# Three latent projections on the raw activations, and a wait moved at a second entry

## The reference, cut to what matters

```
h   = rms_norm(x, mix_norm_g)                       # x: 512 x 1024
cq, ckv, kr, dq, dk, dv, nq, nkv, ng = split(h @ w_in)
qm  = rms_norm(cq,  mla_q_norm_g)  @ mla_w_uq       # cq: 256 columns
kvm = rms_norm(ckv, mla_kv_norm_g) @ mla_w_ukv      # ckv: 128 columns
rms_norm(x, g) = x * rsqrt(mean(x * x) + 1e-6) * g
```

## Time and profile before

| | |
|---|---|
| time, median of three runs | 3802.02 us |
| the profiled execution, its own time | 3804.82 us |
| its span, first to last instruction | 3803.0 us |
| mean granted clock of TensorE | 0.968 |
| PE busy | 3590.6 us (94%) |
| DVE, ACT, POOL busy | 1340.9, 1271.8, 1412.2 us |

### The profile page before, as it was taken

One profiled execution on the slowest core, in us unless ns is written; L12 is line 12 of the kernel. 1 busy time (PEld: TensorE's weight loads), 2 busy tenths in 40 slices (PEclk: granted clock), 3 DMA queues, 4 the chain that ended last, 5 costly groups with the idle time before them and its releaser, 6 DMA issues. The chain is left out here.

```text
span 3803.0 us, 50606 instructions
## 1 busy us (share of the span) xinstructions
PE 3590.6 (94%) x18340; PEld 2846.2 (75%) x18340; DVE 1340.9 (35%) x1910; ACT 1271.8 (33%) x1998; POOL 1412.2 (37%) x756
## 2 busy tenths in 40 slices
PE   7999899999999999899999996999998997879998
PEld 6888675688887888666688885888886874648886
DVE  4233545552325223545542335111115204561112
ACT  4222434542224222334542233312123234234222
POOL 4444333344444444333344442322232440024443
PEclk9999999999999999999999998999998998889999
DMA  4333343233323333333233332222212321013331
GB/s 132 100 94 88 91 120 112 84 89 97 97 85 104 94 99 89 97 111 104 84 94 100 94 100 56 61 67 61 65 51 61 86 75 61 1 44 89 99 94 61
DMA packets 569026, 322.34 MB, mean 85 GB/s; under 512 B 30266, under 2 KB 563360, under 8 KB 568480
## 3 DMA queue, kind: packets, MB, share of 16 engines
q1 hardware_dynamic: 568864, 320.22, 28.9%
HBM read 318.08 MB, written 2.10 MB: 84 GB/s over the span
## 5 line engine op out<-in xcount | busy, mean ns | idle before, releaser
L866 POOL TENSOR_TENSOR w_lo<-w_raw,w_hi 128x1024 fp32r<-128x1024 f32 x516 | 1270.0, 2462 | 2135.1 <-ACT w_hi L911 2135.0
L911 ACT ACTIVATE w_hi<-w_raw 128x1024 fp32r<-128x1024 f32 x516 | 547.0, 1061 | 1847.7 <-PE psum L2143 1733.5
L2143 PE MATMUL psum<-h_hi,w_hi 128*128 128x512 f32 x1296 | 525.9, 406 | 59.5 <-DVE x_lat L1920 27.3
L2143 PE MATMUL psum<-xg_hi,w_hi 128*128 128x512 f32 x1408 | 551.7, 392 | 12.5 <-DVE xg_lo L1470 10.6
L2143 PE MATMUL psum<-xg_lo,w_hi 128*128 128x512 f32 x1408 | 549.0, 390 | 0.0
L2143 PE MATMUL psum<-xg_hi,w_lo 128*128 128x512 f32 x1408 | 548.8, 390 | 0.0
L2143 PE MATMUL psum<-h_lo,w_hi 128*128 128x512 f32 x1296 | 511.2, 394 | 0.0
L2143 PE MATMUL psum<-h_hi,w_lo 128*128 128x512 f32 x1296 | 511.1, 394 | 0.0
L2143 PE MATMUL psum<-a_hi,w_hi 128*128 128x512 f32 x1232 | 433.0, 375 | 4.9 <-DVE a_lo L1587 4.2
L2143 PE MATMUL psum<-a_hi,w_lo 128*128 128x512 f32 x1232 | 432.8, 374 | 0.0
L2143 PE MATMUL psum<-a_lo,w_hi 128*128 128x512 f32 x1232 | 432.3, 374 | 0.0
(11 more groups left out here) (448 smaller groups left out, 4329.7 us busy)
## 6 DMA issues: line engine op xcount, KB each, us to landing
w_raw<-ffn_w SPq DMA_DIRECT2D x120, 512.0 KB, 3.8
w_raw<-ffn_w_gate SPq DMA_DIRECT2D x88, 512.0 KB, 3.8
w_raw<-ffn_w_up SPq DMA_DIRECT2D x88, 512.0 KB, 3.8
ada_raw<-ada_w SPq DMA_DIRECT2D x72, 512.0 KB, 4.6
w_raw<-ffn_w_down SPq DMA_DIRECT2D x64, 512.0 KB, 4.1
w_raw<-w_in SPq DMA_DIRECT2D x60, 512.0 KB, 3.8
w_raw<-ffn_w_down SPq DMA_DIRECT2D x32, 384.0 KB, 3.4
w_raw<-w_out SPq DMA_DIRECT2D x24, 512.0 KB, 4.0
```

The costliest lines, as they stand in the source:

```text
L866: nc.gpsimd.tensor_tensor(w_lo[:, i, :], w_raw[:, i, :], w_hi[:, i, :].bitcast(F32), ALU.subtract).then_inc(lo_ready, 1)
L911: nc.scalar.activation(w_hi[:, pos, :], w_raw[:, pos, :], ACT.Copy).then_inc(hi_ready, 1)
L2143: last = nc.tensor.matmul(dst, w[:, pos, k * P:(k + 1) * P], rhs[g][r](k0 + k), start=k == 0 and m == 0, stop=k == nk - 1 and m == 2)
```

## The change

The mixer's norm gets the arrangement of the FFN: xg_high and xg_low (into a new buffer, mix_lo, that lies over parts of the FFN's buffers which are free by then) run beside the last down tiles. Tiles 0 to 2 (`RAW = 3`) are multiplied from xg. Tiles from the fourth (s = 3) read the normed h_hi and h_lo as before; ACT makes h_hi of chunks 0 to 3 behind tile 0 and of chunks 4 to 7 behind tile 1. The latents are then not normed, so epsilon in their own norms has to be multiplied by mean(x*x) + epsilon: PE adds that to banks 2 and 3 with latent_least times rstd (two matmuls and one) ahead of chunk 7 of tile 0, and the bias becomes epsilon squared. The wait for the parameter loads and for the sum of squares, and the norm's own sum, move to the same place. The clearing of taps moves, since its place now holds xg. In `ffn`, the wait for x_updated is left out in part 0. The rest is renumbering of semaphores.

```diff
 # buffers
+        mix_lo = (over("mix_lo_0", [P, 2, T], zone + 4 * (PARTS[-1][1] * T), F32R), over("mix_lo_1", [P, 6, T], zone + 4 * ((PARTS[0][1] + PARTS[-1][1]) * T), F32R))
+        latent_least = over("latent_least", [P, P], latents_at + 4 * 8 * T)
+        RAW = 3
...
 # ScalarE
-                    nc.scalar.activation(root, sums, ACT.Abs_reciprocal_sqrt, bias=eps[:, 0:1], scale=1.0 / width).then_inc(latent_std.sem, 1)
+                    nc.scalar.activation(root, sums, ACT.Abs_reciprocal_sqrt, bias=eps_square[:, 0:1], scale=1.0 / width).then_inc(latent_std.sem, 1)
...
+                    if s == 0:
+                        norm_high(layer, 1, [(h_hi, 0, T)], cs=range(KD // 2))
                     if s == 1:
...

+                        norm_high(layer, 1, [(h_hi, 0, T)], cs=range(KD // 2, KD))
...
-                late_ffn(layer, FFN_S0[0], FFN_N0[0], lambda c: square(layer, 1, MIX_Y0, c, rows))
-                norm_statistics(layer, 1, MIX_Y0, rows, KD - 1)
-                norm_high(layer, 1, [(h_hi, 0, T)])
+                def mixer_norm(c):
+                    xg_high(layer, 1, MIX_Y0, c, lambda c: layer_gains[:, GAIN_MIX + c:GAIN_MIX + c + 1])
+                    square(layer, 1, MIX_Y0, c, rows)
+
+                late_ffn(layer, FFN_S0[0], FFN_N0[0], mixer_norm)
+                xg_high(layer, 1, MIX_Y0, KD - 1, lambda c: layer_gains[:, GAIN_MIX + c:GAIN_MIX + c + 1])
+                norm_statistics(layer, 1, MIX_Y0, rows, KD - 1, 5)
...
 # VectorE
+                    if v == 0:
+                        nc.vector.memset(taps[:, :, :, NC:CMP_BLOCK], 0.0)
                     place(0, 1, psum[:, 2 + events % 2, :])
...
-                nc.vector.memset(taps[:, :, :, NC:CMP_BLOCK], 0.0)
...
-                    nc.vector.scalar_tensor_tensor(half_square, psum[:, 2 + n, :], width * EPS, half_square, ALU.add, ALU.mult).then_inc(turn_read.sem, 1)
+                    nc.vector.scalar_tensor_tensor(half_square, psum[:, 2 + n, :], width * EPS * EPS, half_square, ALU.add, ALU.mult).then_inc(turn_read.sem, 1)
...
                 def mixer_norm(c):
+                    if c == 0:
+                        nc.vector.memset(latent_least[:], -P * EPS / D)
+                    xg_low(layer, 1, c, lambda c: layer_gains[:, GAIN_MIX + c:GAIN_MIX + c + 1], mix_low(c))
                     if c:
                         norm_add(layer, 1, c, T)
 
                 late_ffn(layer, 0, FFN_S0[0], FFN_N0[0], FFN_Y0[0], mixer_norm)
-                norm_apply(layer, 1, lambda c, g: layer_gains[:, GAIN_MIX + c:GAIN_MIX + c + 1], lats)
+                xg_low(layer, 1, KD - 1, lambda c: layer_gains[:, GAIN_MIX + c:GAIN_MIX + c + 1], mix_low(KD - 1))
+                norm_apply(layer, 1, lambda c, g: layer_gains[:, GAIN_MIX + c:GAIN_MIX + c + 1], lats, 2, bank=5)
...
 # TensorE
-                            if len(groups) > 1:
+                            if len(groups) > 1 and part:
...
-                        last = nc.tensor.matmul(psum[:, b, :], ones[:], flat[:, c * T:(c + 1) * T], start=c == chunks[0], stop=c == chunks[-1])
+                        last = nc.tensor.matmul(psum[:, b, :], ones[:], flat[:, c * T:(c + 1) * T], start=False, stop=c == chunks[-1])
...
-                pe.wait_ge(*params_loaded(layer, PARAMS * 16))
-
-                pe.wait_ge(*x_updated(layer, MIX_Y0))
+                mix = (lambda k: xg_hi[:, k, :]), mix_low
+                mix_ready, normed_rows_ready = rows_ready(layer, 1), rows_ready(layer, 2)
+
+                def first_chunk(k):
+                    if k == KD - 1:
+                        pe.wait_ge(*params_loaded(layer, PARAMS * 16))
+                        pe.wait_ge(*sq_used(layer, 2 * (KD - 1)))
+                        for b, times in ((2, MLA_QR // P), (3, MLA_KVR // P)):
+                            for n in range(times):
+                                nc.tensor.matmul(psum[:, b, :], latent_least[:], rstd[:, 0:T], start=n == 0, stop=False)
+                        norm_sums(layer, 1, [(0, T)], 5)
+                    mix_ready(k)
+
                 for s in range(N_T):
...
-                    dense(s % SLOTS, 0, KD, [lat], [bank_of(s)], rows_ready(layer, 1) if s == 0 else None).then_inc(slot_used, 1)
+                    dense(s % SLOTS, 0, KD, [mix if s < RAW else lat], [bank_of(s)],
+                          first_chunk if s == 0 else normed_rows_ready if s == RAW else None).then_inc(slot_used, 1)
...
-                norm_sums(layer, 1, [(0, T)])
```

More of the change, by code:

```diff
@@ L417, in build @@
         normed_ready = signal("normed_ready", KD)
-        h_hi_ready = signal("h_hi_ready", NORMS * KD)
-        h_lo_ready = signal("h_lo_ready", NORMS * KD, 2)
+        h_hi_ready = signal("h_hi_ready", (NORMS + 1) * KD)
+        h_lo_ready = signal("h_lo_ready", (NORMS + 1) * KD, 2)
         scaled = signal("scaled", 4 * NF)
@@ L562, in slot_of, with mix_low @@
             return layer * (LAYER_SLOTS // SLOTS) + s // SLOTS, s % SLOTS
+        RAW = 3
+        def mix_low(c):
+            return mix_lo[0][:, c, :] if c < 2 else mix_lo[1][:, c - 2, :]
         LAT = [(0, 0, T)]
@@ L939, in norm_statistics, with norm_high @@
                                      scale=(0.5 / D) ** 0.5).then_inc(std_ready.sem, 1)
-            def norm_high(layer, v, groups, shift=None):
-                for c in range(KD):
+            def norm_high(layer, v, groups, shift=None, cs=range(KD)):
+                for c in cs:
                     act.wait_ge(*normed_ready(layer, (v * KD if shift else 0) + c + 1))
@@ L1465, in norm_add, with xg_low @@
                 last.then_inc(sq_used.sem, 1)
-            def xg_low(layer, v, c, gain):
+            def xg_low(layer, v, c, gain, low=None):
                 dve.wait_ge(*h_hi_ready(layer, v * KD + c + 1))
-                nc.vector.scalar_tensor_tensor(xg_lo[:, c, :], x_lat[:, c, :], gain(c), xg_hi[:, c, :].bitcast(F32),
+                nc.vector.scalar_tensor_tensor(xg_lo[:, c, :] if low is None else low, x_lat[:, c, :], gain(c), xg_hi[:, c, :].bitcast(F32),
                                                ALU.mult, ALU.subtract).then_inc(h_lo_ready.sem, 1)
@@ L1502, in _, with norm_apply @@
             nc.vector.tensor_reduce(cond_sum[:], ident[:].rearrange("p (k m) -> p m k", m=COND_M)[:, 0:2, :], AX_X, ALU.add).then_inc(cond_ready, 1)
-            def norm_apply(layer, v, gain, xs, u=None, shift=None, rooted=False):
+            def norm_apply(layer, v, gain, xs, u=None, shift=None, rooted=False, bank=0):
                 u = v if u is None else u
@@ L1509, in norm_apply @@
                     norm_add(layer, v, KD - 1, width)
-                    inverse_root(layer, v, [(o, n) for _, o, n, _, _ in xs])
+                    inverse_root(layer, v, [(o, n) for _, o, n, _, _ in xs], bank)
                 def low(c):
@@ L1844, in mixer_output @@
                     if c >= 1:
-                        xg_low(layer, 2, c - 1, lambda c: layer_gains[:, KD + c:KD + c + 1])
+                        xg_low(layer, 3, c - 1, lambda c: layer_gains[:, KD + c:KD + c + 1])
                     if c >= 2:
@@ L1870, in _ @@
                 mixer_output(layer)
-                xg_low(layer, 2, KD - 1, lambda c: layer_gains[:, KD + c:KD + c + 1])
+                xg_low(layer, 3, KD - 1, lambda c: layer_gains[:, KD + c:KD + c + 1])
                 norm_add(layer, 2, KD - 1, T)
@@ L2192, in gate_and_up @@
                         pe.wait_ge(lo_ready, turn * SLOTS + (SLOTS + 2 * i + u + 1))
-                        dense(2 * i + u, 0, KD, [xg], [psum[:, 3 * i + u, :]], rows_ready(layer, v) if first and u == 0 else None).then_inc(slot_used, 1)
+                        dense(2 * i + u, 0, KD, [xg], [psum[:, 3 * i + u, :]], rows_ready(layer, v + 1 if v else 0) if first and u == 0 else None).then_inc(slot_used, 1)
                         if first and u == 0:
```

## The result

| | before | changed |
|---|---|---|
| median, six executions each | 3799.53 us | 3775.75 us |
| profiled execution | 3804.82 us | 3775.73 us |
| its span, mean granted clock | 3803.0 us, 0.968 | 3773.9 us, 0.973 |

The ratio of the times is 0.9929, 95% interval 0.9915 to 0.9943: 27 us less (22 to 32). The forecast was 3778, in a range of 3764 to 3794.

A forecast was written before the change was run, and what follows sets the result against it. PE's waits were taken as the bound: L1920 at block 2's first projection and gaps at the mixer entry. Gains of 11.2 (two layers) and 13.0 make 24.2 us: 3780.6 profiled, 3778 as median, range 3764 to 3794.

The forecast's parts named there:

- Raw projections: Mixer's tile 0: needs no norm, only xg_hi and xg_lo made beside the last down tiles; chunk 6 ready at 400.1.
- Rival B: Last down tiles: both two-operand DVE instructions are stretched and DVE becomes the bound, 19 us, 3797 us; chance 0.06.
- The parameters are late next: Ahead of chunk 7 of tile 0: PE waits idle for ten parameter loads from 401.0 to 404.7, 3.7 us.
- The clock falls in the wait: Behind the parameter wait: about 5.0 us run at half speed, 2.5 us lost per layer, bounds 0 and 8.6.
- Rival A: Mixer entry: the clock holds through the parameter wait, 2.5 us more gained in each layer, 3773 us; chance 0.20.
- The squares' wait: Latent sum behind tile 1: ACT's split, copy and two squares come late, a new PE wait of 0.9 us.
- Rival C: Tile 3: normed chunks come late, the 1 us margin and then 4 us per layer gone, 3786 us; chance 0.14.
- Mixers: Mixer entry in both layers: 8.1 us less 2.5 for the clock, 5.6 us gained per layer, 11.2 in all.
- Second entry: Block 2's first FFN: part 0 no longer waits for L1920, 13.0 us gained, between 12.1 and 14.2.
- Rival D: Mixers: the clock does not return and PE stays at 1.2 GHz until tile 4, 3819 us; chance 0.04.
- E: Second entry: it gives nothing because another wait takes the place, 3791 us; chance 0.06.
- DVE beside POOL: Last down tiles and normed chunks: POOL's w_lo stretches a two-operand DVE instruction to 2.37 instead of about 0.7 us.

The follow-up runs named there:

- e5: Changed kernel with SyncE issuing the layer's parameter loads about seven tiles earlier; median 3768.6 us, ratio to before 0.9897.
- e4: Changed kernel with 16 more matmuls into an unused bank ahead of the wait for parameter loads; median 3769.2 us, ratio to before 0.9917.
- e2: Changed kernel with the wait for x_updated put back in part 0, so the mixers' part alone; median 3789.9 us, ratio to before 0.9965.
- e6: Changed kernel without the three latent_least matmuls, their epsilon term left out of the output; median 3771.3 us, ratio to before 0.9905.
- e9: The changed kernel itself measured and profiled again, with no edit; median 3777.6 us, ratio to before 0.9925.
- e12: Changed kernel with 28 unused small matmuls in PE's wait ahead of block 2's first FFN; median 3778.2 us, ratio to before 0.9941.
- e8: Changed kernel with least sums, parameter wait and norm's sum behind chunk 7, and ACT's squares ahead of its split; median 3774.0 us, ratio to before 0.9912.
- e13: Kernel before with 118 unused small matmuls ahead of block 2's first FFN; median 3804.3 us, ratio to before 1.0000.
- e1: Kernel before with only the wait for x_updated left out in part 0 of block 2's first FFN; median 3793.3 us, ratio to before 0.9971.
- e10: Kernel before with 100 unused small matmuls ahead of block 2's first FFN; median 3805.5 us, ratio to before 1.0004.
- e3: Changed kernel with the three latent_least matmuls moved ahead of the wait for parameter loads; median 3769.9 us, ratio to before 0.9911.

## Why the prediction was right, step by step

- *Raw projections.* Tile 0 begins at once, chunk 6 is there 0.2 us after PE comes (forecast 400.1 against 399.9), and DVE keeps up with the down tiles. As forecast from the same arrangement at the layer's end. Rival B (DVE the bound, 3797) is refuted by one stretched instruction per tile.
- *The parameters are late next.* Forecast 3.7 us of idle, measured 3.77 and 3.74; e5, which loads them early, shows that no other wait hid behind it but 0.90 for the last rstd. The forecast has its time (the last sum at 401.9, chunk 6 done at 401.0) but did not name it as the next wait.
- *Added matmuls.* Forecast 0.87 us each; at full clock three take 2.68 from their start to the norm sum's (e5, 402.62 to 405.30), 0.89 each.
- *The clock falls in the wait.* Forecast 2.5 us per layer, by e4 2.9 and 2.5. Rival A (it holds) did not occur. But the two numbers behind this step, a fall 3.5 us after PE goes quiet and a return 5.0 after it resumes, are one reading each of something that varies: in the mixers of the five traces with this wait (changed, e2, e6, e9, e12) the fall came after 2.2 to 3.6 us, and in e9's layer 1 the return after 3.0. That 2.5 fits so well is partly luck.
- *The squares' wait.* Forecast 0.9, measured 0.61. Margin of the last normed chunk: forecast 1.0, measured 1.3. Rival C did not occur in the changed kernel, but in e8, which moved one split by 1.8 us, it did: the margin was as thin as forecast.
- *Mixers.* Forecast 5.6 per layer, measured 5.1 and 5.3. Tile 1 begins 16.5 us behind the down projection, forecast 15.9; of the 0.6, 0.4 are the clock in layer 0.
- *Second entry.* Forecast 13.0 between bounds of 12.1 and 14.2, measured 14.07. The mis-sized part is the clock, of which e13 shows how much it was in the kernel before (1.9). I took the middle between "it comes back among the small gaps" and "the gaps hold it down"; it came back at 2312.5, with gaps of 0.92 us still to come, and the last chunk ran at full speed. In e9's trace it did not, and 13.7 is left. Rival D (it does not come back) is refuted in both places, E (another wait takes the place) by e1.
- *Sum.* Forecast 24.2; by place 24.5; by the medians 23.8; by the ratio 27 (22 to 32). The errors (-0.8 in the mixers, +1.1 at the entry) cancel to 0.3, so the mechanism was right, but a fit this close is luck.
- *DVE beside POOL.* The block that was weighed is in the rows once more: where POOL's w_lo meets a two-operand instruction of DVE, it stretches that one, here to 2.39 us, and not the next. In the normed chunks it does so once in each batch, as forecast.

## What to carry to other kernels

When a stage is entered earlier, look at once for what was hidden behind the old wait: here it was ten small parameter loads, and they cost as much (5.5 to 5.7 us per layer, about half as a wait and half as the low clock behind it) as the change gained. Issuing them earlier doubles the mixers' gain with one line (e5). Before a low clock is counted as a loss, ask who sets the pace in that stretch: behind the parameter wait PE did, and it cost 2.5 to 2.9 us; at the second entry DVE did, and it cost nothing until it reached the last chunk. And profiles of two versions should be compared stage by stage, with the same program profiled twice beside them: here two traces of one program lay 13 us apart. Look first at how far a profiled execution lies from its kernel's median.

## What the runs showed of the hardware

- At the mixer's entry the low clock lasted 6.8 us in layer 0 with 5.48 us of least sums behind the wait, and 6.8 us without them (e6). In layer 1 it was 6.8 us in the changed kernel's first trace and 3.4 in its second (e9), with the same work. So its length is not fixed by the program.
- It fell about 2.7 us after PE went quiet in the changed kernel (401.7 to 404.4), 3.5 in the kernel before, 2.6 in e10 (2329.2 to 2331.8), and over all these traces between 2.2 (e12, layer 1: 1527.5 to 1529.8) and 5.3 (e3, second entry: 2291.2 to 2296.5). A quiet of 0.9 us (e3, e5, e13) did not make it fall.
- It returned in a stretch in which PE was gated chunk by chunk (entry of the changed kernel, 2312.5), which the low clock of block 2's mixer had made doubtful. In e9 it fell once more at 2323.2, behind three gaps of 0.92 to 0.93 us.
- In 64 executions of the kernel before, on the chips of e1 to e13, the span ran from 3788.6 to 3810.6 us and the mean clock from 0.971 to 0.965; the correlation is -0.68. Part of a program's scatter goes with its clock. Why the low stretches in attention fall differently from one execution to the next was not settled.
